# Backbone kernel: another order of the input projection pieces, and decays and removal vectors placed with them

## What is computed

```
u = h * (1 + sc1) + sh1
proj = u @ w_in
r, k, v, lo_w, lo_a, lo_g, q, kb, vb, p = split(proj)
decay = exp(-0.606531 * sigmoid(w0 + tanh(lo_w) @ w2))        # two directions
a = sigmoid(a0 + lo_a @ a2)                                   # two directions
kk = k * rw_kk;  kk = kk * rsqrt(max(sum(kk * kk), 1e-24))    # per head
kd = k * (1 + (a - 1) * ka)
scan: S = S * decay - (S kk)(kk * a)^T + v kd^T;  y = S r
bonus = sum(r * (kd0 + kd1) * rk) * v
attention: rms-normed q, kb, rotary on the latent part, vb, cached context keys and values
```

## Time and profile before

| | |
|---|---|
| runs | 1388.66, 1393.7, 1395.04 us (median 1393.7) |
| the profiled execution | 1395.03 us, span 1393.2 us |
| mean granted TensorE clock | 0.888 of full speed (1.00 is 2.4 GHz, 0.50 is 1.2 GHz) |
| busy | PE 1102.8 us (79%), DVE 528.3 (38%), ACT 296.9 (21%), POOL 91.9 (7%) |
| DMA | 217.18 MB, mean 156 GB/s |
| layer 0 | projections 50 to 220 us, attention to 270, scan to about 475 |
| layer 1 | projections 765 to 882 us, attention to 935 |

### The profile page before, as it was taken

The page is one execution under the profiler, slowest core; times in us unless marked ns, Lnnn a source line. Parts: engine busy times, 40 slices in busy tenths (PEclk is TensorE's granted clock), DMA queues, the critical chain, the costliest instruction groups (busy, mean ns, idle before and its releaser), DMA issues. The chain is left out here.

```text
span 1393.2 us, 30493 instructions
## 1 busy us (share of the span) xinstructions
PE 1102.8 (79%) x13450; PEld 693.1 (50%) x13450; DVE 528.3 (38%) x1445; ACT 296.9 (21%) x697; POOL 91.9 (7%) x116
## 2 busy tenths in 40 slices
PE   3689397487878896999945999848878987999933
PEld 2455255277767553333313555538877534333312
DVE  0103016835353526332105330776666254322033
ACT  2012015313121102121202020633232012112112
POOL 2100000000000001111130000000000000111000
PEclk9799797889989997899976999779999997999967
DMA  9853454052616551599935224100000632899521
GB/s 354 225 203 121 193 192 170 1 174 74 235 36 166 171 192 48 181 334 372 363 107 185 85 90 93 31 1 4 4 9 23 222 121 70 290 363 370 211 106 45
DMA packets 145249, 217.18 MB, mean 156 GB/s; under 512 B 20691, under 2 KB 104896, under 8 KB 144672
## 3 DMA queue, kind: packets, MB, share of 16 engines
q1 hardware_dynamic: 132256, 179.32, 38.8%
q0 software_dynamic: 9088, 21.97, 4.6%
q10 hardware_dynamic: 3760, 13.77, 2.6%
HBM read 209.65 MB, written 21.10 MB: 166 GB/s over the span
## 5 line engine op out<-in xcount | busy, mean ns | idle before, releaser
L1355 ACT ACTIVATE region<-bank 128x256 f32<-128x256 f32 (+3 forms) x334 | 142.4, 455 | 387.2 <-PE bank L861 106.7
L1239 PE MATMUL bank<-region 128*32 128x512 f32 x1152 | 173.2, 607 | 2.4 <-ACT region L1355 1.7
L1942 DVE COPY_PREDICATED region<-lev,bank 128x512 f32<-128x512 uint8 (+1 forms) x90 | 61.1, 679 | 123.2 <-PE bank L883 122.7
L1239 PEld LDWEIGHTS bank<-region 128*32 128x32 f32 x1152 | 47.7, 112 | 108.7 <-issue 108.5
L1078 PE MATMUL bank<-u,ring 128*128 128x384 f32 x288 | 96.0, 492 | 0.0
L987 PE MATMUL bank<-ring,cond 128*32 128x128 f32 x1536 | 56.3, 301 | 47.2 <-DMA ring<-in_w_mod 31.6
L1152 PE MATMUL bank<-u,ring 128*128 128x384 f32 x256 | 86.5, 500 | 5.9 <-DVE u L2025 5.9
L1265 PE MATMUL bank<-ring,region 128*32 128x512 f32 x768 | 87.3, 595 | 1.4 <-ACT region L1355 1.4
L987 PEld LDWEIGHTS bank<-ring,cond 128*32 128x32 f32 x1536 | 47.3, 121 | 55.4 <-issue 45.4
L1078 PEld LDWEIGHTS bank<-u,ring 128*128 128x128 f32 x288 | 54.5, 192 | 37.7 <-issue 3.0
L1152 PEld LDWEIGHTS bank<-u,ring 128*128 128x128 f32 x256 | 50.0, 196 | 41.4 <-DVE u L2025 6.3
(11 more groups left out here) (281 smaller groups left out, 1600.2 us busy)
## 6 DMA issues: line engine op xcount, KB each, us to landing
ring<-in_w_mod SPq DMA_DIRECT2D x48, 1024.0 KB
region<-in_moe_w SPq DMA_DIRECT2D x48, 1024.0 KB
ring<-in_moe_w SPq DMA_DIRECT2D x48, 1024.0 KB
ring<-in_w_in SPq DMA_DIRECT2D x20, 768.0 KB
region<-y_rows ACTq DMA_DIRECT2D x6, 1024.0 KB, 9.0
ring<-in_w_in SPq DMA_DIRECT2D x12, 256.0 KB
u_rows<-region ACTq DMA_DIRECT2D x6, 512.0 KB, 2.6
region<-in_bands POOLq DMA_DIRECT2D x2, 1280.0 KB, 7.7
```

The costliest lines, as they stand in the source:

```text
L1239: last = pe.matmul(bank[p % 2][cols, :], xs[:, p % 2, c, cols], of[(p * P + CTILE * q) // CAP][:, c, :], start=(c == 0), stop=(c == KT - 1))
L1355: return act.activation(dst, src, ACT.Copy)
L1942: dve.copy_predicated(quads(xx_m[:, j, lo:8]), lev[:, k, lo // 2:4, :].unsqueeze(2).broadcast_to([P, 4 - lo // 2, 2, C]), quads(bank[j][:, ...
```

## The change

The pieces come in the order low rank inputs, k, q with kb, vb with p, v, r. The list of modulation blocks between them (IN_MODS), the counts at which a slot is free (IN_DONE) and the choice of slots (USED_LATE adds to how late a piece counts as used) are written out for it. On TensorE the low rank outputs stand between the k tiles, the head sums of k after the first q tile, those of q and kb after the first vb tile, the key transpose after the second v tile, the rotary products after the v tiles and after the first r tile, the transposes of v after that; the last tiles are r. ScalarE's front follows the same order. On VectorE the decays and removals leave the attention loop for front; the product with r stays behind the last r copy. GpSimd's new_v waits for front_cp 26 in place of 5.

```
-IN_COLS = ((1536, 512), (2048, 384), (768, 384), (1152, 384), (0, 384), (384, 384))
+IN_COLS = ((1152, 384), (384, 384), (1536, 512), (2048, 384), (768, 384), (0, 384))
+IN_MODS = (1, 1, 3, 2, 0, 1)
+IN_DONE = (3, 18, 25, 32, 35, 41)
+USED_LATE = {("in", 0, 1): 1.5, ("in", 0, 2): 3.5, ("in", 0, 3): 1.5}
...
-        ORDER += [("in", _l, _i)] + ([("mod", 0, MOD_FIRST + _i)] if _l == 0 else [])
-    ORDER += [("mod", 0, i) for i in range(MOD_FIRST + len(IN_COLS), N_MOD)] if _l == 0 else []
+        ORDER += [("in", _l, _i)]
+        if _l == 0:
+            ORDER += [("mod", 0, MOD_FIRST + i) for i in range(sum(IN_MODS[:_i]), sum(IN_MODS[:_i + 1]))]
...
-            slot, turn = min(range(RING), key=lambda i: last[i]), 0
+            slot, turn = min(range(RING), key=lambda i: last[i] + USED_LATE.get(ORDER[last[i]], 0) if last[i] >= 0 else i - RING), 0
...
-                pool.wait_ge(front_cp, FRONT * l + 5)
+                pool.wait_ge(front_cp, FRONT * l + 26)
```

TensorE's new order; feature_tile and token_tile are the eight matmuls of one tile, rest_rows(i) and rest_turn(i) are mod_rows and mod_turn of block i in layer 0 (behind a wait for the block before), lora_out(d) is six low rank outputs, rotate(h) one pair of rotary products, head_sums one sum:

```
+                w = weights(0)
+                tiles_0 = [front_bank() for m in range(3)]
+                for c in range(KT):
+                    pe.wait_ge(u_up, 2 * KT * l + c + 1)
+                    for m in range(3):
...
+                rest_rows(4)
+                w = weights(1)
+                feature_tile(w, 0)
+                rest_turn(4)
+                pe.wait_ge(small_in, 16 * SMALL * (l + 1))
+                lora_out(0)
+                rest_rows(5)
+                feature_tile(w, 1)
+                rest_turn(5)
+                lora_out(1)
...
+                pe.transpose(bank[7][:, 0:P], ctx_k[:, :], ident).then_inc(ckt_mm, 1)
+                feature_tile(w, 2)
+                pe.wait_ge(ckt_cp, l + 1)
+                rest_rows(6)
+                w = weights(2)
+                feature_tile(w, 0)
+                rest_turn(6)
+                pe.wait_ge(kk_sq, l + 1)
+                for j in range(NJ):
+                    head_sums(kr[:, j, :])
+                rest_rows(7)
+                feature_tile(w, 1)
+                rest_turn(7)
+                feature_tile(w, 2)
+                rest_rows(8)
+                feature_tile(w, 3)
+                rest_turn(8)
+                w = weights(3)
+                token_tile(w, 0)
+                rest_rows(9)
+                pe.wait_ge(qk_sq, l + 1)
+                for m in range(4):
+                    head_sums(qk_s[:, m, :])
+                token_tile(w, 1)
+                rest_turn(9)
+                token_tile(w, 2)
+                rest_rows(10)
+                w = weights(4)
+                token_tile(w, 0)
+                rest_turn(10)
+                token_tile(w, 1)
...
+                pe.wait_ge(qk_up, l + 1)
+                pe.transpose(bank[7][:, 0:P], qk[:, 3, 0:P], ident).then_inc(khead_mm, 1)
+                token_tile(w, 2)
+                pe.wait_ge(kh_cp, l + 1)
+                rotate(0)
+                w = weights(5)
+                feature_tile(w, 0)
+                pe.wait_ge(rot_up, 2 * l + 1)
+                rotate(1)
+                pe.wait_ge(front_cp, FRONT * l + 35)
...
+                        last = pe.transpose(dst[:, tc(t)], v_tok[:, t, tc(j)], ident)
...
+                feature_tile(w, 1)
+                pe.wait_ge(rot_up, 2 * (l + 1))
+                rest_rows(11)
+                feature_tile(w, 2)
+                rest_turn(11)
```

VectorE, in front(l):

```
+                dve.wait_ge(front_cp, base + 18)
+                for j in range(NJ):
+                    last = ts(kk_t[:, j, :], k_t[:, j, :], par[:, l, KKP + j:KKP + j + 1], None, ALU.mult)
+                link(last)
+                tt(kr, kk_t, kk_t, ALU.mult).then_inc(kk_sq, 1)
+                for j in range(NJ):
+                    decays(l, 0, j)
+                dve.wait_ge(front_cp, base + 25)
                 tt(qk_s, qk, qk, ALU.mult).then_inc(qk_sq, 1)
+                decays(l, 1, 0)
+                dve.wait_ge(front_cp, base + 30)
                 link(dve.reciprocal(rs, rs))
...
                 last.then_inc(qk_up, 1)
+                decays(l, 1, 1)
+                decays(l, 1, 2)
                 dve.wait_ge(qk_up, l + 1)
                 mark(tt(rs[:, :, P:T], qk[:, :, P:T], rope_cos.unsqueeze(1).broadcast_to([P, 4, DEC]), ALU.mult))
+                removal(l, 0)
+                removal(l, 1)
                 for m in range(2):
                     dve.wait_ge(rot_mm, 2 * l + m + 1)
...
                 tt(qk[:, :, P:T], rs[:, :, P:T], qk_s[:, :, P:T], ALU.add).then_inc(qkr_up, 1)
+                removal(l, 2)
+                dve.wait_ge(front_cp, base + 41)
+                after()
                 for j in range(NJ):
+                    stt(kr[:, j, :], r_t[:, j, :], par[:, l, RKP + j:RKP + j + 1], kr[:, j, :],
+                        ALU.mult, ALU.mult).then_inc(bonus_in, 1)
...
-                    if GRP - 1 <= u < NP - 1:
-                        decays(l, (u - GRP + 1) // NJ, (u - GRP + 1) % NJ)
-                    if u >= NP - 1:
-                        for j in range(2 * (u - NP + 1), min(2 * (u - NP + 1) + 2, NJ)):
-                            removal(l, j)
```

More of the change, by code:

```diff
@@ L108, in item_dmas @@
     kind, _, i = item
-    return 4 if kind == "out" else 7 if kind == "in" and i == 0 else 1 if kind == "over2" else 2
+    return 4 if kind == "out" else 7 if kind == "in" and i == 2 else 1 if kind == "over2" else 2
 def landed_value(n):
@@ L1105, in _, with feature_tile, token_tile @@
-                for d in range(2):
+                    return item_in("in", l, i)[:, 0:KT * n_cols].rearrange("p (c n) -> p c n", c=KT)
+                def feature_tile(w, m):
+                    dst = front_bank()
+                    for c in range(KT):
+                        last = pe.matmul(dst[:, 0:T], w[:, c, tc(m)], u[:, c, :], start=(c == 0), stop=(c == KT - 1))
+                    last.then_inc(front_mm, 1)
+                def token_tile(w, t):
+                    dst = front_bank()
+                    for c in range(KT):
+                        last = pe.matmul(dst[:, 0:NJ * P], u[:, c, tc(t)], w[:, c, :], start=(c == 0), stop=(c == KT - 1))
+                    last.then_inc(front_mm, 1)
@@ L1116, in _, with rotate @@
                             pe.matmul(dst[:, 0:T], w2[d * HD:(d + 1) * HD, tc(j)], lo[d * HD:(d + 1) * HD, :],
                                       start=True, stop=True).then_inc(front_mm, 1)
+                def rotate(half):
+                    for m in range(2):
+                        last = pe.matmul(bank[7][:, m * DEC:(m + 1) * DEC], rot, qk[:, 2 * half + m, P:T], start=True, stop=True)
+                    last.then_inc(rot_mm, 1)
+                w = weights(0)
+                tiles_0 = [front_bank() for m in range(3)]
@@ new lines, in _ @@
+                for c in range(KT):
+                    pe.wait_ge(u_up, 2 * KT * l + c + 1)
+                    for m in range(3):
+                        last_c = pe.matmul(tiles_0[m][:, 0:T], w[:, c, tc(m)], u[:, c, :], start=(c == 0), stop=(c == KT - 1))
+                        if c == KT - 1:
+                            last_c.then_inc(front_mm, 1)
+                rest_rows(4)
[3 more added lines that the diff above has]
+                pe.wait_ge(small_in, 16 * SMALL * (l + 1))
```

183 lines of the change are left out of this document (73 added, 110 removed).

## The result

The changed kernel takes 1312.54 us (median of 4 runs, 1302.33 to 1316.08); the kernel before, on the same chip, 1394.37 (4 runs, 1388.66 to 1396.59). The ratio is 0.9407, with a 95% interval from 0.9345 to 0.9469. The forecast was 1307, its range 1297 to 1336: right in sign, 5.5 us too low, inside the range. The profiled execution took 1310.06 us with a span of 1308.3 and a mean granted clock of 0.914.

The account below looks back on a forecast made before the run. It took load waits to bound layer 0's projections and VectorE to bound attention. 1395.0 less 43.2 (order), 22.8 and 21.3 (attentions), loads of layer 1 at 0, gave 1307.7, stated as 1307 us, range 1297 to 1336.

Parts of the forecast that it names:

- part 2: Projections of layer 0: the new order of pieces gains 43.2 us, 27.5 of it waits on modulation blocks.
- the start: First projection matmul of layer 0 at 42.7 in place of 49.97, 7.3 us gained.
- part 1: Attention: decays and removals moved off VectorE's loop there gain 21.3 us in layer 0 and 22.8 in layer 1.
- Rival B: Attention in both layers: the clock stays at 1.2 GHz throughout, total about 1330 us; chance 0.14.
- The move under the projections at no cost: Projections: VectorE's moved decays and removals fit between its projection work, margin 2 to 8 us, cost nothing.
- The sign set for it: Projections of layer 1: longer than 117 us would show the forecast wrong.
- GpSimd's copies: Start of attention: three copies beside the first maxima cost 0, bounds 0 and 1.7 us a layer.
- part 3: Layer 1's loads beside the reload of y_rows: taken at 0, best 5 us less, worst 3 more.
- C: Layer 0: the fill or 512 column piece catches a block, a 5 to 22 us stall, total 1313 to 1330; chance 0.22.
- D: Whole kernel slower than before: loads fall behind their slots throughout, 1398 us or more; chance 0.02.
- E: Projections: moved VectorE work stays in a queue TensorE waits for, at most 30.8 us a layer back, up to 1369; chance 0.02.

Follow-up runs that it names:

- the run with the late products: The changed kernel with the three receptance multiplies moved behind units 3 to 5 of attention; 1305.78 us, ratio 0.9388.
- the run with the order alone: The changed kernel with decays, removals and receptance multiply back in the attention loop, only pieces and loads in new order; 1358.56 us, ratio 0.9757.
- The run with the fill early: The changed kernel with the zero fill of y_rows issued when the keys are complete, not after the key copy; 1332.42 us, ratio 0.9575.

## Why the prediction was right, and where it was off

The sign and the size came from three terms, and each was found where it was put.

**The waits in the projections of layer 0** (part 2): forecast -35.9 behind the start, measured -36.0. The fill as the cause of the 22.28 is shown both ways, by moving it out in the kernel before and in again in the changed one.

**The attentions** (part 1): -22.8 and -21.3 forecast, -23.3 and -21.3 measured. Under it two errors cancel. The clock was forecast back 8 us after the first scores; it came back after 12.7 in layer 0 and 11.2 in layer 1. On the other side a unit at 2.4 GHz takes 2.47 us (192.14 to 194.61) and not 2.8, and the waits are short. That they cancel so closely is luck. I had left the first units at the lower clock because they were so before; that this was worth 6 us for two layers, and that it could be had, I did not see. Rival B, the slow clock throughout, did not happen: it fell away with VectorE's gaps. What was said for it, 20 us at the lower clock in both layers, was true of layer 1 alone; in layer 0 of the kernel before the longest such stretch is 13.6 us (229.0 to 242.6).

**The move under the projections at no cost** held: no row of TensorE in either layer's projections waits for VectorE, with 2 us to spare at the rotation, as worked out. The sign set for it, projections of layer 1 longer than 117 us, did come up, at 117.8; but it was set too tight, since the kernel before has 117.2 and the other executions 116.2 to 117.9.

GpSimd's copies were taken at 0. They now lie beside the first maxima of layer 0 (VectorE's timeline after, with GpSimd's row first):

```profile
180.35 1.71 POOL L666 COPY region<-cst 128x512 f32<-128x512 f32 x3 [25.70 <-DVE region L1889]
180.64 0.33 DVE L1925 TENSOR_SCALAR region<-region 128x2 f32<-128x2 f32 x1
...
181.33 0.20 DVE L1925 TENSOR_SCALAR region<-region 128x2 f32<-128x2 f32 x1
...
183.17 0.17 DVE L1925 TENSOR_SCALAR region<-region 128x2 f32<-128x2 f32 x1
```

The two maxima beside the copies read PSUM and take 0.41 us each, against 0.42 away from the copies. The two small TENSOR_SCALARs are lengthened, 0.2 us in all, and each ends 0.02 to 0.03 us after one of the three copies does (180.95 and 181.50). The Trainium skill (SBUF — State Buffer, "SBUF: two separate sides") has VectorE, in some of its operations, and GpSimd hold a shared port pair for a whole instruction while the other waits, and the trace agrees. It costs so little because the copies end where normalising begins, at 182.05. In the run with the late products they lie across a normalising pair, which takes 0.97 in place of 0.75. The 1 to 3 us that the prediction gives by the rule were too much.

**The step that was mis-sized is part 3, layer 1's loads at 0.** At the first scores of layer 0 the run with the order alone is 42.3 ahead, where 43.2 were forecast; but of these it keeps 31.5 in its total. Part of the loss is located: from the reload's issue to the first projection the profiled execution takes 1.4 us more than before, the six executions of the new order 1 to 4 more, where I took 0 with 3 as the upper end. Holding the pieces takes this away and some 4 us more, a cost that the old order had too. The landings agree: 15.4 against 13.9, and 9.4 once the pieces are held. The rule that I weighed there, of the Trainium skill (DMA: Bandwidth & Descriptors, "Queues, rings and completion order"), is that queues take turns by packets; that longer runs then take more of the engines from the reload is my reading of it. The old order with its first piece in long runs points this way, 17.2 in place of 13.9. But there the next pieces also go out sooner, so whether it is the length of the runs or the bytes on the way, no run separates.

The other 2.7 us of that stage's 4.1 lie ahead of the reload's issue and come and go whether the pieces are held or not. The 6 to 7 us more that the run with the order alone lost lie in the scan and in output and routing, where nothing was edited; no cause is shown for them, and in the changed kernel these stages gained 2.9.

A smaller miss is the start. I put it at 42.7, with TensorE following u; it is 44.95, after 4.28 of idle for the first piece. In three other runs with the new order it is 42.1 to 42.4, in the other five 44.6 to 45.5, so the forecast was one of two values that occur. With the start's 2.3 and the 4.1 of the stage with the reload the sum would have been too low by 6.4; the scan, routing and the rest gave 4.1 of it back, with nothing edited in them, and that is luck too.

**The rivals.** C, a new stall on a block, did not come: block 7 was used 9.2 us after its issue. The run with the fill early shows what it costs, 18.9 us, and that the block has to be in before the fill goes out. SP was forecast to be kept 17 us by the six head DMAs; it was 9.3, so block 6 had 14.8 us where I gave it 9. D and E show in no row.

## What to carry over

When a wait on a load is far longer than its bytes need, look at what any other queue issued in the same microseconds: here the fill's place behind the last urgent load was worth 16 to 20 us, while the DMA engines as a whole were busy 0.38 of the time. Look also at what a prefetch shares the engines with: holding one until an urgent reload had landed was worth 6 us and more. An engine that fills a stretch while TensorE starves should have its movable work put under the stretches where TensorE is full; check each hand-over against the tile that covers it. Then look at the first idle microseconds of the new stage, because what follows them may run at the lower clock for longer than they last.

## What the runs showed of the hardware

- TensorE's clock fell after an idle stretch of 2.27 us and stayed at the lower level through nearly unbroken work: for 10.3 us in layer 0 of the changed kernel and its repetition, for 6.9 in two other runs with the same stretch. After an idle stretch of 1.34 it was 3.4 us in one run and 10.3 in another. In layer 1 it was 6.9 in all six of them, after 2.54 or 1.41 us. With 2.20 us of matmuls in the stretch's place it stayed at 2.4 GHz, although TensorE does more work.
- The fill holds up a block that is already under way: one issued 0.8 us ahead of it was used 27.2 us after its issue, one issued 1.5 us ahead 27.5, where 8 to 9 us do without it. Its own 3 MB take 24.4 to 25.6 us in all twelve traces, with the DMA engines busy 0.38 of the time when nothing else moves.
- How long SP is kept by the six DMAs with 256-byte runs differs with the place: 16.5 and 17.3 us at the head of the old order, 9.2 to 9.5 between the keys and the queries, 19.8 to 21.9 beside the reload (15.8 and 16.2 in the old order), 12.9 to 13.1 behind it. What sets it, no run shows.
- A small TENSOR_SCALAR of VectorE (128x2, 0.17 us alone) that ran into one of GpSimd's copies (0.6 us each) ended 0.02 to 0.03 us after that copy, in all 26 meetings in eight traces; reductions that read PSUM did not change (0.41 us).
